# Rotation partners exchanged by DMA: issued by SyncE between weight loads instead of by ScalarE

## The reference, cut to what matters

```python
def moba_mixer(xn, w_qkv, w_o, cos, sin):
    B, S, _ = xn.shape                       # S = 256, 16 heads of 64
    qkv = (xn @ w_qkv).reshape(B, S, 3, N_HEADS, HEAD_DIM)
    q = apply_rope(qkv[:, :, 0], cos, sin)
    k = apply_rope(qkv[:, :, 1], cos, sin)
    o = moba_attention(q, k, qkv[:, :, 2])   # causal softmax(q k / 8) v here
    return o.reshape(B, S, N_HEADS * HEAD_DIM) @ w_o

def apply_rope(x, cos, sin):
    half = x.shape[-1] // 2
    x1, x2 = x[..., :half], x[..., half:]
    c = cos[None, :, None, :]
    s = sin[None, :, None, :]
    return jnp.concatenate([x1 * c - x2 * s, x2 * c + x1 * s], axis=-1)
```

## Time and profile before

| | us |
|---|---|
| median of 3 runs | 1131.89 |
| lowest, highest run | 1131.02, 1132.49 |
| profiled execution | 1129.82 |
| its span, first to last instruction | 1128.0 |
| TensorE busy | 1095.8 |
| VectorE busy | 720.7 |
| ScalarE busy | 591.8 |
| GpSimd busy | 136.5 |

### The profile page before, as it was taken

One profiled execution on the slowest core, in us unless ns is written; L12 is line 12 of the kernel. 1 busy time (PEld: TensorE's weight loads), 2 busy tenths in 40 slices (PEclk: granted clock), 3 DMA queues, 4 the chain that ended last, 5 costly groups with the idle time before them and its releaser, 6 DMA issues.

```text
span 1128.0 us, 20227 instructions
## 1 busy us (share of the span) xinstructions
PE 1095.8 (97%) x8264; PEld 968.3 (86%) x8264; DVE 720.7 (64%) x1221; ACT 591.8 (52%) x970; POOL 136.5 (12%) x160
## 2 busy tenths in 40 slices
PE   8999999999999999899999999999999999999998
PEld 7787888766777989689898999999997799999997
DVE  5546567276535667766865686766676666776664
ACT  5332666444334557756565555544563646454454
POOL 0000010054020000423332100000014311000000
PEclk9999999999999999999999999999999999999999
DMA  9732212177421434035453455455452234545551
GB/s 373 308 112 76 75 38 75 40 278 279 151 75 38 150 130 141 1 121 189 150 178 113 153 188 221 153 184 200 174 187 78 103 122 144 196 182 187 189 192 49
DMA packets 25964, 169.07 MB, mean 150 GB/s; under 512 B 3344, under 2 KB 3728, under 8 KB 6288
## 3 DMA queue, kind: packets, MB, share of 16 engines
q1 hardware_dynamic: 24336, 165.67, 40.6%
q10 hardware_dynamic: 1536, 2.10, 0.7%
HBM read 164.62 MB, written 1.05 MB: 147 GB/s over the span
## 4 chain that ended last, share of the span: by engine, by line
PE 84%; DVE 6%; ACT 4%; DMA 2%; issue 2%; POOL 2%; SPq 0%; ACTq 0%; DVEq 0%; POOLq 0%
PE bank L425 24%; PE bank L426 23%; PE bank L427 23%; DVE wlo L419 2%; ACT whi L404 2%; PE bank L1521 2%; PE bank L471 1%; PE bank L1387 1%; DMA PROJ<-in_stream 1%; PE bank L1531 1%; PE bank L1541 1%; PE bank L1414 1%; PE bank L1405 1%; PE bank L1262 1%; DVE STAT L1564 1%
## 5 line engine op out<-in xcount | busy, mean ns | idle before, releaser
L425 PE MATMUL bank<-OPH,whi 128*128 128x256 f32 (+1 forms) x1716 | 524.1, 305 | 5.5 <-ACT AV L2774 2.2
L426 PE MATMUL bank<-OPL,whi 128*128 128x256 f32 (+1 forms) x1716 | 514.8, 300 | 0.0
L427 PE MATMUL bank<-OPH,wlo 128*128 128x256 f32 (+1 forms) x1716 | 514.8, 300 | 0.0
L419 DVE TENSOR_TENSOR wlo<-raw,whi 128x1024 fp32r<-128x1024 f32 x256 | 305.3, 1235 | 105.7 <-ACT whi L404 105.7
L425 PEld LDWEIGHTS bank<-OPH,whi 128*128 128x128 f32 x1716 | 328.0, 191 | 26.8 <-issue 9.5
L426 PEld LDWEIGHTS bank<-OPL,whi 128*128 128x128 f32 x1716 | 328.2, 191 | 12.0 <-issue 1.4
L427 PEld LDWEIGHTS bank<-OPH,wlo 128*128 128x128 f32 x1716 | 328.1, 191 | 10.9
L404 ACT ACTIVATE whi<-raw 128x1024 fp32r<-128x1024 f32 x256 | 255.7, 1049 | 100.7 <-PE bank L427 100.0
L425 PE MATMUL bank<-whi,OPH 128*128 128x256 f32 (+1 forms) x272 | 89.2, 328 | 0.0
L426 PE MATMUL bank<-wlo,OPH 128*128 128x256 f32 (+1 forms) x272 | 87.2, 321 | 0.0
L427 PE MATMUL bank<-whi,OPL 128*128 128x256 f32 (+1 forms) x272 | 87.1, 320 | 0.0
(11 more groups left out here) (290 smaller groups left out, 1193.3 us busy)
## 6 DMA issues: line engine op xcount, KB each, us to landing
raw<-in_stream SPq DMA_DIRECT2D x147, 1024.0 KB, 4.8
PROJ<-in_stream SPq DMA_DIRECT2D x5, 1024.0 KB, 14.8
X<-in_x_in SPq DMA_DIRECT2D x4, 512.0 KB, 5.8
PROJ<-PROJ ACTq DMA_DIRECT2D x32, 64.0 KB, 4.1
C<-in_con SPq DMA_DIRECT2D x1, 1413.5 KB, 9.8
out<-PROJ SPq DMA_DIRECT2D x4, 256.0 KB, 2.0
WST<-in_w_s SPq DMA_DIRECT2D x2, 256.0 KB, 5.1
PROJ<-in_last_gain SPq DMA_DIRECT2D x1, 512.0 KB, 6.5
```

The costliest lines, as they stand in the source:

```text
L419: nc.vector.tensor_tensor(c.w[1][:, part], c.raw[:, part], c.w[0][:, part].bitcast(F32), ALU.subtract).then_inc(*raises(c.lo[h]))
L425: nc.tensor.matmul(out, w[0], x[0], start=start, stop=False, skip_group_check=skip)
L426: nc.tensor.matmul(out, w[0], x[1], start=False, stop=False, skip_group_check=skip)
L427: return nc.tensor.matmul(out, w[1], x[0], start=False, stop=stop, skip_group_check=skip)
```

## The change

The four DMAs of a swap leave `step`, where ScalarE ran them, and become a function `swap(e, i)` with the same two waits (the group's eviction, and the spare buffer's release by an earlier add). The eight `Rs` items leave the plan. SyncE calls `swap` inside its loop over the chunks: `swap_before` maps the chunk of job index + 7 to the group, and the swap is issued ahead of that chunk's wait and load. So q0 stands ahead of load +7, k0 ahead of +8, q1 of +10, k1 of +11, q2 of +12, k2 of +13, q3 of +14 and k3 of +15. Number, size and addresses of the transfers stay.

```diff
+            def swap(e, i):
+                for point in due(e, ready(i), t[i].empty):
+                    e.wait_ge(*point)
+                for h in range(4):
+                    e.dma_start(blocks_of(t[i].mem)[32 * h:32 * h + 32], group(i)[32 * (h ^ 1):32 * (h ^ 1) + 32]).then_inc(
+                        *raises(swapped(i)[h], 16))
+
             def step(e, who, n):
                 what, i = n
-                if what == "swap" and who == "act":
-                    for point in due(e, ready(i), t[i].empty):
-                        e.wait_ge(*point)
-                    for h in range(4):
-                        e.dma_start(blocks_of(t[i].mem)[32 * h:32 * h + 32], group(i)[32 * (h ^ 1):32 * (h ^ 1) + 32]).then_inc(
-                            *raises(swapped(i)[h], 16))
...
+        first_qkv = len(chunks)
         qkv = moba_qkv(op0.block, [("moba_columns",)], high)
...
+        swap_before = {first_qkv + qkv.at[name] + 7: i for i, name in enumerate(f"{c}{g}" for c in "qk" for g in range(4))}
...
-                F("k1"), A("k1"), Rs(5), s_(1), V_("k1"), n_(1),
+                F("k1"), A("k1"), s_(1), V_("k1"), n_(1),
...
             for c in chunks:
+                if c.i in swap_before:
+                    rt.swap(sp, swap_before[c.i])
                 if c.before is not None:
                     for point in due(sp, c.before.lo if c.before.split else c.before.used):
                         sp.wait_ge(*point)
```

More of the change, by code:

```diff
@@ L2564, in pool_step @@
                         *raises((f"{name}_times_cos", i)))
-            s.pool_step = pool_step
+            s.pool_step, s.swap = pool_step, swap
             s.take_step, s.pe_step, s.step = take_step, pe_step, step
@@ L3217, in program @@
         F, A, V_ = (lambda name, what=what: [(qkv_jobs, (what, qkv.at[name]))] for what in ("fill", "act", "dve"))
-        Rs, Ra, Rb = (lambda i, what=what: [(rt, (what, i))] for what in ("swap", "turn", "add"))
+        Ra, Rb = (lambda i, what=what: [(rt, (what, i))] for what in ("turn", "add"))
         s_, n_, t_, w_ = (lambda p, names=names: [(at, (what, p)) for what in names] for names in
@@ L3221, in program @@
         W = lambda i, ks: [(beside, (i, ks))]
-        plan = [[(qkv_jobs, ("together", (qkv.at["q0"], qkv.at["k0"])))], A("q0"), Rs(0), V_("q0"), A("k0"), Rs(4), V_("k0"),
+        plan = [[(qkv_jobs, ("together", (qkv.at["q0"], qkv.at["k0"])))], A("q0"), V_("q0"), A("k0"), V_("k0"),
                 [(mix0, 0)], F("v0"), [(mix0, 1)], A("v0"), Ra(0), Ra(4), Rb(0), Rb(4), V_("v0"), [(mix0, 2)],
-                F("q1"), A("q1"), Rs(1), s_(0), V_("q1"), n_(0),
-                F("k1"), A("k1"), Rs(5), s_(1), V_("k1"), n_(1),
[L3226 to L3229, removed]
+                F("q1"), A("q1"), s_(0), V_("q1"), n_(0),
+                F("k1"), A("k1"), s_(1), V_("k1"), n_(1),
+                F("q2"), A("q2"), Ra(1), Ra(5), t_(0), Rb(1), Rb(5), V_("q2"),
+                F("k2"), w_(0), A("k2"), s_(2), t_(1), V_("k2"), n_(2),
+                F("q3"), w_(1), A("q3"), s_(3), Ra(2), Ra(6), Rb(2), Rb(6), V_("q3"), t_(2), n_(3),
+                F("k3"), A("k3"), s_(4), t_(3), V_("k3"), n_(4),
                 F("v1"), A("v1"), s_(5), Ra(3), Ra(7), t_(4), Rb(3), Rb(7), V_("v1"), n_(5),
```

## The result

The change makes the kernel slower. The median of four runs is 1140.99 us against 1132.19 us of the kernel before beside it, a ratio of 1.0088 (95% interval 1.0074 to 1.0102), 8.8 us. Run again on another chip, the changed kernel had 1141.74 against 1130.05 us, 1.0097 (1.0082 to 1.0113). The forecast was slower by 4.6 us, at 1136.5 us: the direction and the place were right, the size was half of what came. The kernel before had 1132.19 us beside the first measurement and 1130.05 to 1130.59 us beside all later ones, and the changed kernel nearly the same time in both, so the loss is 9 to 12 us rather than exactly 8.8.

A forecast was written before the change was run, and what follows sets the result against it. TensorE, busy 97% of the span, was taken as the bound; late swaps delay adds, splits and loads in three steps, 1.1, 3.45, then 4.6 us late in all. Added to the 1131.89 us median: 1136.5 us, range 1132.0 to 1141.5.

The forecast's parts named there:

- The landing of a swap is what ends last at that place: Before pair 0's scores: k0's last piece lands at 536.37 and VectorE turns k0 0.02 us later.
- Ahead of load +7 means right behind load +6: SyncE's order: swaps start right behind the preceding load; q0, k0 and k2 start 4 us later, each behind a 1 MB load.
- The 3.1 us from the landing to the end of the second add: VectorE's time from a swap's landing until its adds are over, read from the earlier trace as 3.1 us.
- The issue work on this queue costs the loads about nothing: SyncE: 32 added issues at 0.61 us each barely delay loads, since the next load waits for a VectorE split anyway.
- I take 6.4: Time from a load's issue to the landing of the swap behind it: 6.4 us, with bounds 4.2 and 8.1.
- the lag counts three times: Rounds of k0, k1 and k2: with lag g the lateness is 4.6 + 3 x (g - 6.4) us.
- q3 and k3: I cost them at nothing more: Last swaps, behind the scores of pair 5, already 4.6 us late: no further lateness added.
- ScalarE's 0.7 us at k0's eviction: Removing ScalarE's issues brings k0's eviction 0.7 us earlier and shrinks TensorE's 1.54 us factor wait by up to 0.7.
- The scores of pair 4 wait less: TensorE at 578.14: these scores wait less while the transposes of pair 3 move by 4.6 us.
- the 3 us forecast: TensorE's wait before the transposes of pair 3 rises from 0.38 to about 3 us.
- whose rule gave 1131.2 us: Rival: swaps as timely as before, only ScalarE's 0.7 us left, 1131.2 us; chance 0.16 together with a shorter lag.
- 0.76 for slower: Whole kernel: chance 0.76 of being slower by over 0.2%, against 0.16 within 0.2% and 0.08 faster.

The follow-up runs named there:

- q0_six: Changed kernel with q0's swap alone one load earlier, k0 staying behind load +7: 1140.36 against 1130.05 us of the kernel before, 1.0093.
- six_k0: Changed kernel with only q0's and k0's swaps one load earlier (job index + 6): 1136.23 against 1130.59 us of the kernel before, 1.0051.
- seven_k0: Changed kernel with q0 and k0 left at job index + 7, the other six swaps one load earlier: 1134.56 against 1130.41 us before, 1.0039.
- clock_kept: Changed kernel plus added matmuls of ones by ones while TensorE waits: 1140.20 against 1130.59 us of the kernel before, 1.0084.
- six_all: Changed kernel with all eight swaps one load earlier (job index + 6): 1132.04 against 1130.59 us of the kernel before, 1.0010.
- both_ahead_six: All swaps on SyncE, q0 and k0 both ahead of load +6, other six at job index + 6: 1129.61 against 1130.05 us before, 1.0000.
- six_k2: Changed kernel with only q2's and k2's swaps one load earlier: 1139.67 against 1130.05 us of the kernel before, 1.0074.
- both_ahead_act: Kernel before with only q0's and k0's swaps on SyncE, both ahead of load +6, other six on ScalarE: 1129.84 against 1130.41 us, 0.9992.
- front_of_load: Changed kernel with each swap issued ahead of the load it had followed, after that load's wait: 1133.55 against 1130.59 us before, 1.0022.

## Why the prediction was right in kind and wrong in size

- "The landing of a swap is what ends last at that place": right. The waits before the scores of pairs 0, 2 and 4 in the changed kernel are waits for the adds, and moving swaps one load forward took 7 us and more away.
- "Ahead of load +7 means right behind load +6", and starts 4 us later: right, the chain shows each swap 0.4 to 0.6 us behind a load. q0 started 3.8 us later, k0 4.2 us, k2 11 us, the last by the lateness of the rounds before it.
- The 3.1 us from the landing to the end of the second add: right, it was 3.0 us at k0, k1 and k2.
- "The issue work on this queue costs the loads about nothing": right for load +7, which went 0.1 us later than before. But an issue was not 0.61 us throughout: 0.80, 0.81 and 1.03 us stand in the chain above, and 2.60 us in the kernel without k2's step.
- "I take 6.4" for the lag, the time from a load's issue to the landing of the swap behind it: this is the step that failed, a term that was mis-sized in a mechanism that was right. It was 8.7 us at k0 (531.57 to 540.23), 6.5 at k1 (557.99 to 564.54) and 8.0 at k2 (574.16 to 582.13). The sum with these lags in the places of 6.4 gives 4.6 + 2.3 + 0.1 + 1.6 = 8.6 us, against 9.2 measured at k2's adds. The two groups that gave 6.4 were picked as undisturbed because no load followed them; but they were undisturbed on the other side as well, since no load had gone for 9 us and more before theirs. In the new order loads +7 and +12 go 3.4 and 4.3 us after the load before, with a swap in between, and load +10, whose lag was 6.5, 5.3 us after its neighbour. The kernel before had a row for nearly this case: load +6 went 4.3 us behind load +5, with q0's pieces in between, and k0's last piece, the third behind that load, landed 8.1 us after it (528.26 in the earlier trace rows to 536.37). I used that row for the old time of k0 and not for the lag. Over the traces of all runs it holds on the whole: where a swap began within 0.6 us of a load's issue and that load had followed its neighbour within 4.3 us (28 groups), the lag was 7.1 to 9.1 us, with a median of 8.0; with 4.7 us or more between the loads (48 groups) it was 6.3 to 8.5 us, with a median of 6.8. Why some of the second kind are long too, as k3 in the kernel before with 8.1 us, and why q0_six gave back only 0.8 us, stays open.
- The step "the lag counts three times" held: in the table the lateness grows in each round, and six_k0 and seven_k0 add up to the whole within their intervals.
- "q3 and k3: I cost them at nothing more": wrong as a reason. In the kernel without k2's step k3's round stalls TensorE for 1.90 us; in the changed kernel it was covered by the slow TensorE.
- The clock was not in the sum. TensorE was 9.2 us late at the transposes of pair 3 (588.59 against 579.4 for the first of them) and 11.1 us late at the scores of pair 5 (597.64 against 586.58): 1.9 us more, in a stretch with a granted clock of 0.51. It looks like the price of the dip; clock_kept shows that it isn't one by itself, since with the clock held the late k3 takes nearly the same. That the sum with the measured lags, 8.6 us, comes so close to the 8.8 us of the medians is in part luck: it leaves out these 2 us, and the profiled executions differ by 11.4 us.
- ScalarE's 0.7 us at k0's eviction, and the shorter wait for the factor: right (the eviction 0.9 us earlier, 1.54 us became 0.6), and worth nothing at the end.
- "The scores of pair 4 wait less": wrong. They waited 1.89 us for k2's adds; the wait before the transposes of pair 3 was 2.44 us, near the 3 us forecast.
- Of the Trainium skill I cited "DMA: Bandwidth & Descriptors", section "Issuing engines are not separate DMA queues", whose rule gave 1131.2 us. That issuing elsewhere saves only sequencer time agrees with six_all and both_ahead_six, 1.0010 and 1.0000: at the same place in time, the engine that issues hardly matters. What decided here was the swap's place in SyncE's order, behind a wait and a load.
- The chances: 0.76 for slower was borne out, and 1140.99 us lies just inside the range of 1132.0 to 1141.5, at its upper end; the 1141.74 us of the second measurement would have been outside. The likeliest value should have gone by the lag of the row with the same traffic ahead, not by the two best.

## What to carry to other kernels

When a transfer moves to a queue that issues in order, its start is no longer set by its data but by the wait in front of it: write down the time of the release of each neighbour, not the place in the program. If what the transfer feeds also releases the neighbour's next wait, one delay comes back once for each round; look for that loop before costing the first step. And take the duration of a transfer from rows with the same traffic ahead of them as in the new order, and put the less favourable row in the middle of the estimate.

## What the runs showed of the hardware that was not expected

- An issue on a queue is not a constant. Behind a 1 MB load four 64 KB pieces took 2.4 to 4.5 us to issue on SyncE, single pieces up to 1.80 us (six_all) and one 2.60 us (six_k2), where 0.6 us is usual.
- The last of four such pieces landed 6.3 to 8.7 us after the issue of the load in front of them in the changed kernel; in both_ahead_act the last of eight pieces behind no load since 524 us landed 2.9 us after its own issue.
- Behind a wait of TensorE of 4.36 us, and again behind two of 1.89 and 2.44 us with 0.9 us of scores between them, the granted clock was at 0.50, the level of 1.2 GHz, for several microseconds. In front_of_load a single wait of 2.74 us was followed by 0.50 as well (542.8 to 548 us). Holding it at 1.00 with added matmuls brought no measurable time, because VectorE's chain set the pace.
